# Reordering index scores by query block, and an earlier, thinner top-k selection, in an fp32 two-block transformer kernel

## The reference, cut to what matters

```python
idx_scale = (N_IDX_HEADS * IDX_DIM) ** -0.5            # 16 heads of 64
def one_block(i):                                      # 128 queries, T = 512 keys
    wb = block_slice(w_idx, s0) * idx_scale
    idx_logits = einsum('bqhd,bsd->bqhs', qib, k_idx)
    score = einsum('bqh,bqhs->bqs', wb, relu(idx_logits))
    score = where(causal, score, -inf)
    _, sel = lax.top_k(score, top_k)                   # top_k = min(256, T // 4) = 128
    ... softmax attention of 8 heads over the selected keys
```

## Time and profile before

| | |
|---|---|
| median of 3 runs | 2655.59 us (2651.74 to 2656.82) |
| the profiled execution, its own time | 2656.64 us |
| its span | 2654.8 us |
| TensorE's granted clock over the span | 0.991 of full |
| PE busy | 2601.8 us (98%) |
| DVE busy | 1347.7 us (51%) |
| ACT busy | 754.3 us (28%) |

### The profile page before, as it was taken

How to read it: one execution, slowest core, us unless ns; L and a number is a source line. 1 busy time by engine, 2 the same in 40 slices (tenths; PEclk the granted TensorE clock), 3 DMA queues, 4 the chain that set the end, 5 groups by cost and what they waited for, 6 DMA issues and landing times.

```text
span 2654.8 us, 33223 instructions
## 1 busy us (share of the span) xinstructions
PE 2601.8 (98%) x12356; PEld 2100.3 (79%) x12356; DVE 1347.7 (51%) x1959; ACT 754.3 (28%) x1032; POOL 368.5 (14%) x306
## 2 busy tenths in 40 slices
PE   8999999988999999999999999999999999999998
PEld 6888887655488888888888888888887768888887
DVE  7666655577657643364434434444226663433334
ACT  4222232355532321331111111322322452322223
POOL 1111123000021010131001001103001104110112
PEclk9999999989999999999999999999999999999999
DMA  6454433110035333333333332233331013233331
GB/s 190 145 143 142 139 107 94 38 37 17 1 118 151 111 97 93 102 89 95 96 94 95 95 95 67 61 110 89 86 111 41 13 50 96 81 95 95 95 91 67
DMA packets 358032, 241.21 MB, mean 91 GB/s; under 512 B 14768, under 2 KB 356144, under 8 KB 357936
## 3 DMA queue, kind: packets, MB, share of 16 engines
q1 hardware_dynamic: 357936, 239.92, 30.7%
HBM read 237.79 MB, written 2.10 MB: 90 GB/s over the span
## 4 chain that ended last, share of the span: by engine, by line
PE 93%; DVE 3%; ACT 2%; issue 1%; POOL 0%; DMA 0%; DVEq 0%; SPq 0%; ACTq 0%; POOLq 0%
PE PS L816 23%; PE PS L823 23%; PE PS L818 23%; PE PS L793 4%; PE PS L796 4%; PE PS L794 4%; PE PS L1284 2%; PE PS L1075 1%; PE PS L1276 1%; PE PS L1114 1%; PE PS L1121 1%; PE PS L984 1%; PE PS L748 1%; DVE VA L1691 1%; PE PS L1085 0%
## 5 line engine op out<-in xcount | busy, mean ns | idle before, releaser
L816 PE MATMUL PS<-NH,WH 128*128 128x512 f32 (+1 forms) x2112 | 615.4, 373 | 3.6 <-DVE WL L1670 1.8
L818 PE MATMUL PS<-NH,WL 128*128 128x512 f32 (+1 forms) x2112 | 613.5, 372 | 0.0
L823 PE MATMUL PS<-NL,WH 128*128 128x512 f32 (+1 forms) x2112 | 585.4, 372 | 0.0
L1670 DVE TENSOR_TENSOR WL<-RAW,WH 128x2048 fp32r<-128x2048 f32 x189 | 471.9, 2497 | 109.7 <-ACT WH L1315 109.3
L1315 ACT ACTIVATE WH<-RAW 128x2048 fp32r<-128x2048 f32 x189 | 361.7, 1914 | 498.9 <-PE PS L823 491.7
L823 PEld LDWEIGHTS PS<-NL,WH 128*128 128x128 f32 x2112 | 385.4, 189 | 71.3 <-POOL NL L2303 0.7
L818 PEld LDWEIGHTS PS<-NH,WL 128*128 128x128 f32 x2112 | 385.3, 188 | 70.8
L816 PEld LDWEIGHTS PS<-NH,WH 128*128 128x128 f32 x2112 | 382.8, 188 | 73.6 <-issue 5.4
L2261 POOL CAST HH<-VA 128x512 f32 (+2 forms) x88 | 60.4, 686 | 1305.0 <-DVE VA L1831 1305.0
L1389 ACT ACTIVATE SA<-PS 128x512 f32<-128x512 f32 x104 | 62.1, 597 | 628.9 <-PE PS L823 595.7
L816 PE MATMUL PS<-HH,WH 128*128 128x512 f32 (+1 forms) x820 | 238.1, 371 | 0.0
(11 more groups left out here) (345 smaller groups left out, 2631.2 us busy)
## 6 DMA issues: line engine op xcount, KB each, us to landing
RAW<-in_ffn_w_in SPq DMA_DIRECT2D x88, 512.0 KB, 5.0
MW<-in_w_mod SPq DMA_DIRECT2D x72, 512.0 KB, 3.5
RAW<-in_w_in SPq DMA_DIRECT2D x70, 512.0 KB, 4.3
RAW<-in_w_gate SPq DMA_DIRECT2D x44, 512.0 KB, 4.0
RAW<-in_w_up SPq DMA_DIRECT2D x44, 512.0 KB, 5.3
RAW<-in_w_down SPq DMA_DIRECT2D x32, 512.0 KB, 4.2
RAW<-in_ffn_w_out SPq DMA_DIRECT2D x32, 512.0 KB, 4.2
RAW<-in_w_out SPq DMA_DIRECT2D x16, 512.0 KB, 4.0
```

The costliest lines, as they stand in the source:

```text
L816: pe.matmul(outs[half][x], w[half][0], xh(k), start=i == 0, stop=False)
L818: pe.matmul(outs[half][x], w[half][1], xh(k), start=False, stop=False)
L823: last = pe.matmul(outs[half][x], w[half][0], xl(k), start=False, stop=i == kn - 1)
L1670: dve.tensor_tensor(WL[1 - s][:, :], RAW[1 - s][:, :], WH[1 - s][:, :].bitcast(F32), ALU.subtract).then_inc(w_lo, 1)
```

## The change

`INDEX` now takes query block 1 with its 16 heads, then block 2, then block 3, so the sum of q = 1 is complete after unit 15 (projection block 7), of q = 2 after unit 31, of q = 3 after unit 47. The table of places and all slots and banks stay. Each sum now waits for the one just before it (same `BIAS` row), unless it is a block's first. The selection is moved ahead: its generator waits for the 16 sums of its query block, and `selected(k)` takes k steps. 10 steps stand behind the sums of projection block 8, 3 after its split, 4 behind the sums of block 9, 4 more before DVE waits for that block, 5 after it, 16 behind the sums of units 32 to 47: 42 in all. In the attention one step is left in each round, before `masked`, and a second one only in rounds 16 to 23.

```diff
--- before.py
+++ after.py
@@ -418,7 +418,7 @@
 
 
 
-        INDEX = [(1 + i % 3, 2 * hp + i % 2) for hp in range(IDX_HEADS // 2) for i in range(6)]
+        INDEX = [(q, h) for q in range(1, NT) for h in range(IDX_HEADS)]
         IN_W = {6: ((0, 1), (0, 6), (1, 1), (1, 4)), 7: ((0, 1), (0, 6), (1, 1), (1, 4)),
                 8: ((0, 1), (0, 4), (1, 0), (1, 2), (1, 5)), 9: ((0, 1), (0, 5))}
         IX0 = {n: sum(2 * len(IN_W[m]) for m in IN_W if m < n) for n in range(6, 11)}
@@ -1921,11 +1921,34 @@
                 keys = (q + 1) * P
                 acc = BIAS[:, q - 1, 0:keys]
                 dve.wait_ge(ix_relu, n + 1)
-                if n >= 3:
-                    dve.wait_ge(ix_acc, n - 2)
+                if h:
+                    dve.wait_ge(ix_acc, n)
                 dve.scalar_tensor_tensor(out=acc, in0=ix_relu_slot(n)[:, 0:keys], scalar=WI[:, q, h:h + 1],
-                                         in1=acc if n >= 3 else CM[:, (NT - 1 - q) * P:T],
+                                         in1=acc if h else CM[:, (NT - 1 - q) * P:T],
                                          op0=ALU.mult, op1=ALU.add).then_inc(ix_acc, 1)
+
+            def select():
+
+                for q in range(1, NT):
+                    dve.wait_ge(ix_acc, IDX_HEADS * q)
+                    acc = BIAS[:, q - 1, 0:(q + 1) * P]
+                    for r in range(TOPK // 8):
+                        own.inc(dve.max(M8[:, :], acc))
+                        n = own.n
+                        yield
+                        dve.wait_ge(dve_s, n)
+                        own.inc(dve.match_replace(acc, M8[:, :], acc, 3 * NEG * 1e7))
+                        n = own.n
+                        yield
+                        dve.wait_ge(dve_s, n)
+                    own.settle(dve, dve.tensor_scalar(acc, acc, 2 * NEG * 1e7, NEG, ALU.is_gt, ALU.mult))
+
+            selection = select()
+
+            def selected(n):
+
+                for _ in range(n):
+                    next(selection, None)
 
             for n in range(10):
                 b = w_in_b + n
@@ -1936,8 +1959,11 @@
                     own.settle(dve, dve.memset(VAP[:, :, :, :], 0.0))
                 for i in range(IX0.get(n, 0), IX0.get(n + 1, 0) if n in IN_W else 0):
                     index_sum(i)
+                    if n >= 8:
+                        selected(1)
                 if n == 9:
                     norm_inverse(norm_q)
+                    selected(4)
                 dve.wait_ge(pe_done, b + 1)
 
                 for i, half in enumerate(COPIED[n], COPY0[n]):
@@ -1957,6 +1983,8 @@
                 dve.sem_inc(psum_free, 1)
                 if n < 9:
                     split(1 - s, b + 1)
+                if n >= 8:
+                    selected(3 if n == 8 else 5)
                 for i, (kind, half, dst) in enumerate(ITEMS[n], ITEM0[n]):
                     dve.wait_ge(rope_mm, i + 1)
                     o = B[4 + i % 2]
@@ -1992,21 +2020,7 @@
                 if n == SPLIT_PJ:
                     split(v_b % 2, v_b)
                 index_sum(n)
-
-            def select():
-
-                for q in range(1, NT):
-                    acc = BIAS[:, q - 1, 0:(q + 1) * P]
-                    for r in range(TOPK // 8):
-                        own.inc(dve.max(M8[:, :], acc))
-                        n = own.n
-                        yield
-                        dve.wait_ge(dve_s, n)
-                        own.inc(dve.match_replace(acc, M8[:, :], acc, 3 * NEG * 1e7))
-                        n = own.n
-                        yield
-                        dve.wait_ge(dve_s, n)
-                    own.settle(dve, dve.tensor_scalar(acc, acc, 2 * NEG * 1e7, NEG, ALU.is_gt, ALU.mult))
+                selected(1)
 
             dve.wait_ge(ix_acc, len(INDEX))
             dve.wait_ge(v_out, NT)
@@ -2053,7 +2067,6 @@
                 i = B[4][:, :] if g < 4 else B[4][:, :].rearrange("p (h q) -> p h q", h=4)
                 dve.tensor_tensor(heads_out(g, NL), i, heads_out(g, NH).bitcast(F32), ALU.subtract).then_inc(at_o, 1)
 
-            selection = select()
             ROUNDS = TOPK // 8
 
             assert all(32 + HA * q - AHEAD > ROUNDS * q for q in range(1, NT))
@@ -2070,7 +2083,8 @@
                 if u + AHEAD < len(UNITS):
                     masked(u + AHEAD)
                 if u >= 0:
-                    next(selection, None)
+                    if 16 <= u < 24:
+                        selected(1)
                     if u % PER_GROUP == 1 and u > 1:
                         heads(u // PER_GROUP - 1)
             heads(NG - 1)
```

## The result

The changed kernel took 2659.51 us (median of 19 runs, 2656.86 to 2662.12), the kernel before 2655.59 us beside it (19 runs). The ratio is 1.0016, 95% interval 1.0009 to 1.0023: 4.2 us slower (2.4 to 6.1), inside the 0.2% that was called no change, and 1.7 us from the forecast. The profiled execution took 2661.53 us. Its page has nearly the busy times and chain shares of before: the case is one of a few microseconds in a stretch of 260, between the first index pair and the output projection.

What follows compares the result with a forecast made beforehand. PE was taken to bound the kernel, with ACT in parts of the attention and DVE a close second. Terms -2.8 + 0 + 4.0 + 1.0 = +2.2 us on 2655.6 gave 2657.8 us, range 2650 to 2665 us.

Steps and rivals of the forecast that it cites:

- Pairs of equal width: Projection blocks 6 to 9: an index pair costs its wider member, so 15 equal pairs gain 2.8 us.
- Chained sums at no cost: Projection blocks 6 to 9: sums that each wait for the one before cost nothing extra.
- the second of my two reasons: DVE idles longer in blocks 6 and 7, and a step between sums covers the wait in blocks 8 and 9.
- 26 early steps at no cost: Selection steps in and just after projection blocks 8 and 9: cost 0, or 0.8 us without later cover.
- Late part +4.0: Sixteen 512-key index units with steps, before the attention: DVE's backlog delays the first `KB` copy by 4.0 us.
- Attention +1.0: Attention rounds: two steps in rounds 16 to 23 cost 1.3 us, rounds 24 to 27 return 0.3; net loss 1.0.
- signs of being wrong: First `KB` copy before 566 or after 571 us, or DVE's selection in the chain of attention rounds 16 to 47.
- Rival 1, the clock falls in the new wait: PE's wait before the `KB` copy: short fall costs 1.8 us, long up to 6.5; chance 0.13, long 0.10.
- Rival 2, full lengths: DVE between 547 and 571 us: each operation takes its whole duration, +6.6 instead of +4.0, 2660.4 us; chance 0.12.
- Rival 3, DVE the bound: Attention: DVE was the bound, so +1.0 becomes -4, giving 2652.8 us, or 2649.8 at best; chance 0.10.
- Rival 4, pairs don't gain: Projection: weight loads set 256-key pairs, gain only 0.5 us, sum +4.5, 2660.1 us; chance 0.10.
- The named marks: 256-key pair 0.60 us, last block's end 2.8 earlier, last sum 565.5, `KB` copy 568, same distances from group 4.

Runs made afterwards that it cites:

- The last experiment: Kernel before with index units cycling through the query blocks pair by pair, each pair of one width, selection left in the attention: 2651.10 us, ratio 0.9983.
- second profile of before: The kernel before, unchanged, profiled once more on another chip: 2651.61 us.
- order alone: Kernel before with only the index units' order (and its sum waits) changed, all 96 selection steps left in the attention: 2655.27 us, ratio 1.0003.
- after (again): The changed kernel, unchanged, profiled once more on another chip: 2660.24 us.
- fillers: Extra PE products at waits around the attention's start: with only the order changed 2654.91 us, in the changed kernel 2658.94, with query blocks also descending 2655.31.
- chained waits: Kernel before with every index sum waiting for the one just before it instead of the third last: 2655.78 us, ratio 1.0006.
- descending blocks: Kernel with only the index order changed, its query blocks now taken wide first and narrow last: 2655.64 us, ratio 1.0002.
- the kernel with the doubles at rounds 0 to 7: Changed kernel with its eight rounds of two selection steps at 0 to 7 instead of 16 to 23: 2657.95 us, ratio 1.0014.

## Why the prediction was right, point by point

The direction and the time came out: 2657.8 us forecast, 2659.51 measured, and each term of the sum within 0.1 to 1.2 us of its stage. One term was put at nothing and wasn't, the clock. The forecast's +2.2 lies just below the measured interval (2.4 to 6.1), and a range 15 us wide would have held much worse sums, so it is the stages that speak for the mechanism and not the total.

- **Pairs of equal width: right, low by 0.3.** The bound from the maximum of the columns held; 0.25 us of fixed part with three passes gives 0.57, and the row says 0.55. The last experiment shows it apart from the block order.
- **Chained sums at no cost: right in the kernel after, for the second of my two reasons.** Where two sums stand side by side, as in blocks 6 and 7, DVE has idle time; where it has none, a step stands between two sums. Bare, they are not free: 0.86 us for a sum of 0.74. The Trainium skill (VectorE: DVE Perf Modes, The DRAIN you can't avoid), which I had weighed against unchained sums at 0.54, describes these better, and says in the same place that an operation which is not held starts earlier, as the unchained ones did: behind a wait on its neighbour a sum starts no earlier than the neighbour's full length, here 0.1 us later still. The same six sums took 3.26 us with the waits three back and 4.22 with them on the neighbour.
- **26 early steps at no cost: right** within 0.6 us of one profile against another (90.8 against 90.2), or 1.0 if only the late part is looked at (below).
- **Late part +4.0: right in mechanism.** The `KB` copy came 36.6 and 36.3 us after block 9, the forecast's 36.3. The rise against before is 4.3 and 5.2, because the second profile of before was 1.2 us faster than the row I counted from. My sum has a slip of 0.2: 547.5 + 20.8 + 2.2 is 570.5, not 570.8. Not foreseen were DVE's waits for ACT, 1.1 and 2.05 us, made up in part by shorter steps (20.5 for 20.8). The experiments divide the rise: order alone 0.4 to 1.6 (32.7 against 32.3 and 31.1), the early steps up to 1.0 (33.7), the 16 late ones 2.6 to 2.9.
- **Attention +1.0: right** for DVE's part. Group 2 lost 1.44 at full clock (forecast 1.3), groups 0 to 1 and 2 to 4 gave back 0.23 and 0.29 to 0.41 (forecast 0.3, put wholly into rounds 24 to 27): 0.9 in all in the second profile. One of my signs of being wrong was the selection in the chain of rounds 16 to 47. It is there, in the kernel after and in rounds 16 to 23: the sign was badly put, since a loss of 1.3 us by DVE in those rounds means just that. In the kernel before no selection line stands among those listed from 629 to 695 us.
- **Rival 1, the clock falls in the new wait: it happened, as the short fall.** The first profile of after has 0.68 over 565 to 570 us, 0.8 us to group 0 more than before. The second has its fall at the attention's start instead, for 2.8 us. PE's wait for the first `KB` copy is the new one, first before, then after (again):

```profile
567.53 0.45 PE L1054 MATMUL PS<-NH,WH 128*64 128x512 f32 x1 [0.79 <-DVE KB L2021]
```

```profile
568.75 0.45 PE L1054 MATMUL PS<-NH,WH 128*64 128x512 f32 x1 [1.53 <-DVE KB L2035]
```

  The Trainium skill (TensorE: Matmul & The Clock Gate, Why this matters for your kernels) has idle gaps between bursts followed by half rate. The first profile agrees, with waits of 1.30 and 1.54 us; the second, with waits of 1.33 and 1.53, was at full clock until 582 us, and in the order-only kernel the fall at 577 us came behind 3.32 of 4 us busy and 1.21 of 2 us busy, nothing like the empty wait I had looked at. Yet the wait and the fall go together over the kernels. In all six profiles without fillers in which PE waited 1.2 to 1.6 us for that copy the clock fell between 566 and 592 us, and group 0 came after 28.9 to 31.3 us. In the four with 0.7 to 0.8 (before twice, chained waits, pairs cycled) it did not fall there, and it was 28.2 us; nor did it fall there in the kernel with descending blocks, which has no such wait, or in the three with fillers. How the wait leads to a fall up to 16 us later is not shown.
- **Rival 2, full lengths: false** beside a step (0.66 and 0.47 from start to start), true of bare chained sums. Its +6.6 also needs the value loads of 0.08 to 0.09 us; the durations that I listed give +5.8. **Rival 3, DVE the bound: false**, DVE's 11.37 fell to 9.90 of 12 us and the stage to group 1 moved by 0.2 to 0.3 us. **Rival 4, pairs don't gain: false.**
- **The sum.** +2.2 was forecast and 4.2 (2.4 to 6.1) measured. The term that I put at nothing is the clock: I priced its fall as a rival with 0.13, while a fall worth 0.8 and 2.8 us behind the new wait or at the attention's start is in both profiles of after and in neither of before. The granted clock averages 0.9887 over the 19 runs of after, and 0.9905 to 0.9909 over the runs of before that stand beside the experiments. How much of the 4.2 us it makes stays open: with fillers the kernel after has 0.9901, and its ratio is still 1.0013. The named marks held: pair 0.55 (0.60), block 9's end earlier by 2.2 and 3.1 (2.8), last sum's end 563.6 (565.5) and `KB` copy 566.3 (568) in a span whose first index pair came 2.6 us earlier for a fall that before had at 465 us, same distances from group 4 on but for the last `heads`.

## What to carry to other kernels

Two row-tiled matmuls that run side by side cost the wider one, so pair equal widths first and choose the order of the pairs for the engine behind them. That reordering, with the waits that go with it and nothing else of this change, was the only version measured as faster. Work moved ahead is free only into an engine's idle time: the same step cost next to nothing in the projection, a third of itself beside a chained sum, all of itself as the second one, and 1.6 us in eight rounds where it worked on longer rows than before. And an engine at 95% busy was still not the bound: read who stands in the chain before paying to relieve it.

## What the runs showed of the hardware

- **A chained operation on DVE costs more than its length.** Six sums, each waiting for the one before it: 0.59 us apart at 256 keys for 0.48 of length ((3.43 - 0.48) / 5), 0.86 apart at 512 for 0.74. A step on another row of `BIAS` between them starts 0.66 after the sum, and the next sum 1.13 after the one before it, 0.27 later than without the step of 0.55.
- **The clock's falls move, and in sets.** Every profile has at least one stretch at half clock that begins between 524 and 540 us, 3 to 20 us long. The rest differs: the first profile of after has falls at 566, 640 and 722 us, the second at 464 and 582, and the kernel with the doubles at rounds 0 to 7 at 464 and 582 too. Those that a stage shows apart are worth 0.8 to 3.0 us. A difference of this size in one stage of one profile says nothing until it is seen twice.
